# Hybrid attention layer: an early bias line, late weights a stage ahead, 128-row key blocks in B, A's mask on VectorE, one weight ring

## What is computed

```python
h  = rmsnorm(x, norm_g)                       # (1024 + 64) x 2048
qa, ka, va, qi, wi, ki, za, qb, kb, vb, zb, ga, gb = split(h @ w_in)
# A: 8 heads of 128, 2 kv heads. An indexer (16 heads of 64) scores every admissible key;
#    each query attends to its top 256 (prompt) of the keys; the sample also reads 2048 cached keys
score = sum_h relu(qi . ki) * wi ;  idx = top_k(score, n_sel)
oa = softmax(qa . ka[idx] * D_A**-0.5 + bias[t5_bucket(s - t)]) @ va[idx]
# B: 16 heads of 64, window of 128 keys back from the 64-frame chunk's start, plus the own chunk,
#    with a learned sink per head in the softmax, and the same T5 bias
ob = swa(qb, kb, vb, sinks, bias)
m  = sigmoid(ga) * ((oa * silu(za)) @ w_br_a) + sigmoid(gb) * ((ob * silu(zb)) @ w_br_b)
y  = rmsnorm(x + m @ w_out, final_g)
```

## Time and profile before

| | us |
|---|---|
| median of 3 runs (lowest, highest) | 3295.89 (3295.25, 3297.86) |
| the profiled execution | 3299.35 |
| its span | 3297.6 |
| PE busy | 3118.6 (95%), 17861 matmuls |
| DVE, ACT, POOL busy | 1321.4 (40%), 923.3 (28%), 1032.3 (31%) |
| mean granted clock of TensorE | 0.976 of full |

### The profile page before, as it was taken

One profiled execution on the slowest core, in us unless ns is written; L12 is line 12 of the kernel. 1 busy time (PEld: TensorE's weight loads), 2 busy tenths in 40 slices (PEclk: granted clock), 3 DMA queues, 4 the chain that ended last, 5 costly groups with the idle time before them and its releaser, 6 DMA issues. The chain is left out here.

```text
span 3297.6 us, 48426 instructions
## 1 busy us (share of the span) xinstructions
PE 3118.6 (95%) x17861; PEld 2950.5 (89%) x17861; DVE 1321.4 (40%) x2491; ACT 923.3 (28%) x1902; POOL 1032.3 (31%) x773
## 2 busy tenths in 40 slices
PE   6999999999999999889999799987998999899997
PEld 6999999999999989889999788876778999878776
DVE  6001563755567549900000256444873211120512
ACT  5111122121323131111111355444653111031423
POOL 1222211212222322222222366435762222143453
PEclk8999999999999999999999899997999999999998
DMA  4222222223232322153222553346545333263443
GB/s 159 66 79 77 73 65 73 71 68 84 71 100 74 98 73 80 54 141 99 80 80 82 147 152 101 93 106 153 118 97 178 104 125 105 79 224 98 150 160 105
DMA packets 432085, 341.57 MB, mean 104 GB/s; under 512 B 37244, under 2 KB 391644, under 8 KB 428428
## 3 DMA queue, kind: packets, MB, share of 16 engines
q1 hardware_dynamic: 398992, 275.97, 30.4%
q10 hardware_dynamic: 32956, 63.77, 6.0%
HBM read 264.25 MB, written 75.48 MB: 103 GB/s over the span
## 5 line engine op out<-in xcount | busy, mean ns | idle before, releaser
L466 POOL TENSOR_TENSOR w_in_tile_lo<-w_in_tile_raw,w_in_tile_hi 128x512 fp32r<-128x512 f32 x316 | 411.0, 1302 | 1391.4 <-ACT w_in_tile_hi L486 1391.4
L594 PE MATMUL banks<-h_early_hi,w_in_tile_hi 128*128 128x384 f32 x2496 | 639.4, 337 | 3.8 <-POOL w_in_tile_lo L466 3.8
L594 PE MATMUL banks<-h_early_hi,w_in_tile_lo 128*128 128x384 f32 x2496 | 636.5, 336 | 0.0
L594 PE MATMUL banks<-h_early_lo,w_in_tile_hi 128*128 128x384 f32 x2496 | 635.9, 336 | 0.0
L486 ACT CAST w_in_tile_hi<-w_in_tile_raw 128x512 fp32r<-128x512 f32 x316 | 196.3, 621 | 1254.1 <-PE banks L594 1128.5
L594 PEld LDWEIGHTS banks<-h_early_hi,w_in_tile_hi 128*128 128x128 f32 x2496 | 434.5, 188 | 13.0 <-issue 5.1
L594 PEld LDWEIGHTS banks<-h_early_hi,w_in_tile_lo 128*128 128x128 f32 x2496 | 434.8, 188 | 0.0
L594 PEld LDWEIGHTS banks<-h_early_lo,w_in_tile_hi 128*128 128x128 f32 x2496 | 434.4, 188 | 0.0
L761 DVE MAX8 top<-score 128x8 f32<-128x384 f32 (+6 forms) x224 | 247.2, 1103 | 33.0 <-DVE score L764 1.1
L764 DVE MATCH_REPLACE8 score<-top,score 128x384 f32<-128x384 f32 (+6 forms) x224 | 243.0, 1085 | 0.0
L2327 POOL TENSOR_TENSOR w_out_tile_lo<-w_out_tile_raw,w_out_tile_hi 128x512 fp32r<-128x512 f32 x128 | 173.7, 1360 | 215.4 <-ACT w_out_tile_hi L2337 215.4
(11 more groups left out here) (255 smaller groups left out, 5047.5 us busy)
## 6 DMA issues: line engine op xcount, KB each, us to landing
w_in_tile_raw<-in_w_in SPq DMA_DIRECT2D x440, 256.0 KB, 2.9
w_out_tile_raw<-in_w_out SPq DMA_DIRECT2D x128, 256.0 KB, 3.1
product<-spill ACTq DMA_DIRECT2D x46, 544.0 KB, 3.4
u_b<-product SPq DMA_DIRECT2D x32, 544.0 KB, 6.1
product<-spill ACTq DMA_DIRECT2D x32, 384.0 KB, 2.5
merged<-u_b ACTq DMA_DIRECT2D x16, 544.0 KB, 7.5
x_rows<-in_x_prompt SPq DMA_DIRECT2D x8, 1024.0 KB, 5.2
b_q_raw<-product SPq DMA_DIRECT2D x32, 256.0 KB, 4.8
```

The costliest lines, as they stand in the source:

```text
L466: pool.tensor_tensor(s.w_lo[:, q, :, :], s.w_raw[:, q, :, :], s.w_hi[:, q, :, :].bitcast(F32), ALU.subtract).then_inc(lo_made, 1)
L594: last = pe.matmul(ps[0:m, 3 * slot + c, 0:w], w_[:, q, kq, 0:m], tokens, start=(k == 0 and w_ is s.w_hi and h_ is s.h_hi), stop=(k == KT ...
```

## The change

1. The event `"bias line"` stands after the first tile of `QA`, with its two table DMAs issued at `"prompt keys"`. From the rows of A's heads their farthest value is subtracted (softmax doesn't change by a constant per row), so far keys need no bias: the far loads (L1011, L1356) go. The line is stored at once, on ACT's queue. What stood with it (the sample's mask, cache copies, the load of the sample's keys and values) is the new event `"load the sample"`, one tile later than `"bias line"` was.
2. The first two late tiles of each attention stage are loaded in the stage before (the second's DMAs at its end, `load_rest`), and the splits of the second wait for no load. The splits keep their points.
3. B's second key block has 128 rows: `prob` is padded with zero columns from 192 to 256 and the missing rows of `v_raw` with zeros; `values_lo` and the cast become one operation each.
4. The identity matmuls with A's mask go. Far pieces add the bf16 mask on DVE in place of the scalar; for near pieces POOL adds mask and bias beforehand, into a ring of 4 (`mask_near`, 64 operations in the prompt), or once in place (sample, at point 2). `load_mask` waits for `max_made` in place of `logits_done`.
5. All weight tiles use one set of buffers (`w_tile`). `attend_b` loads and splits merge's first branch tile after its last gate store, and `merge` loads and splits output's first four w_out tiles and loads its first two rows of m (`m_raw` becomes shared).
6. The fp32r and bf16 copies of the identity are not made.

```diff
     plan = [(QI, 2, "copy", None), "natural", (QI + 2 * P, 6, "copy", None), "prompt keys",
-            (QA, 2, "copy", None), (QA + 2 * P, 1, "copy", 2), (QA + 3 * P, 3, "copy", None),
+            (QA, 1, "copy", None), "bias line", (QA + P, 1, "copy", None), (QA + 2 * P, 1, "copy", 2), (QA + 3 * P, 3, "copy", None),
...
-            (GA + 20 * P, 2, "early", NB), (QB + 9 * P, 1, "copy", None), (GA + 22 * P, 8, "early", None),
-            "bias line", (GA + 30 * P, 2, "early", None),
+            (GA + 20 * P, 2, "early", NB), (QB + 9 * P, 1, "copy", None), (GA + 22 * P, 9, "early", None),
+            "load the sample", (GA + 31 * P, 1, "early", None),
...
                 elif what == "prompt keys":
+                    sp.dma_start(table, rel_bias).then_inc(consts_in, 16)
+                    sp.dma_start(hot, one_hot).then_inc(consts_in, 16)
...
-                elif what == "bias line":
+                elif what == "load the sample":
                     store_mask(NB)
-                    sp.dma_start(table, rel_bias).then_inc(consts_in, 16)
-                    sp.dma_start(hot, one_hot).then_inc(consts_in, 16)
...
-            load_tile(n_tiles, 0, 0, late_tile)
+            for k in range(2):
+                load_tile(n_tiles + k, 0, 0, late_tiles[k])
+            for q in range(QUARTERS):
+                sp.wait_ge(w_in_q[q], 16 * (n_tiles + 1))
...
+                    act.wait_ge(line_out, 3)
+                    act.dma_start(s.lines[:], line.unsqueeze(1).to_broadcast([H_A + H_B, P, RELS])).then_inc(line_stored, 16)
+                elif what == "load the sample":
...
+                    dve.memset(farthest, 0.0).then_inc(line_out, 1)
+                    dve.wait_ge(line_out, 1)
                     dve.wait_ge(line_done, 1)
-                    dve.tensor_copy(line, ps[0:H_A + H_B, 7, 0:RELS]).then_inc(line_out, 1)
-                    dve.wait_ge(line_out, 1)
+                    dve.tensor_copy(farthest[0:H_A, :], ps[0:H_A, 7, 0:1]).then_inc(line_out, 1)
+                    dve.wait_ge(line_out, 2)
+                    dve.tensor_scalar(line, ps[0:H_A + H_B, 7, 0:RELS], farthest, None, ALU.subtract).then_inc(line_out, 1)
...
+    def quarters(self, p, ahead, ready, end):
+
+        return range(*(max(ready, min(end, self.steps_before[x] // 4 + ahead)) if x >= 0 else ready for x in (p - 1, p)))
+
+    def load_quarter(self, sp, n):
+        t, q = divmod(n, QUARTERS)
+        sp.wait_ge(self.w_lo_made, n - 7)
+        src = self.w_in[0, q * KQ * P:(q + 1) * KQ * P, self.columns[t]:self.columns[t] + P]
+        sp.dma_start(self.s.w_raw[:, q, :, :], src.rearrange("(k p) c -> p k c", p=P)).then_inc(self.w_loaded[q], 16)
...
+        for n in self.quarters(p, 7, 2 * QUARTERS, QUARTERS * len(self.columns)):
+            self.load_quarter(sp, n)
+
+    def load_rest(self, sp):
+        end = QUARTERS * len(self.columns)
+        for n in range(min(end, self.steps_before[-1] // 4 + 7), end):
+            self.load_quarter(sp, n)
+        for q in range(QUARTERS):
+            sp.wait_ge(self.w_loaded[q], 16 * (len(self.columns) - 2))
...
+        for n in self.quarters(p, 4, QUARTERS, self.split):
             t, q = divmod(n, QUARTERS)
             act.wait_ge(self.w_used, n - 3)
-            act.wait_ge(self.w_loaded[q], 16 * t)
+            if t > 1:
+                act.wait_ge(self.w_loaded[q], 16 * (t - 1))
...
-                sp.wait_ge(logits_done, first_chunk[first_of(b - 1)])
+                sp.wait_ge(max_made, first_of(b - 1))
...
+            def mask_near(n):
+                b, u = units[n]
+                wide = min(NEAR, width[b])
+                if n == 0:
+                    pool.wait_ge(masks_set, 2)
+                if n in (0, PER):
+                    pool.wait_ge(table_in[n // PER], 16)
+                if u == 0 and b >= 2:
+                    pool.wait_ge(mask_in[b % 2], 16 * (b // 2))
+                if n >= RING:
+                    pool.wait_ge(max_made, n - RING + 1)
+                pool.tensor_tensor(near_masked[:, n % RING, 0:wide], near[:, u, NEAR - wide:NEAR], mask[:, b % 2, width[b] - wide:width[b]],
+                                   ALU.add).then_inc(near_made, 1)
...
+                mask_near(p)
+            mask_near(START)
             for n in range(len(units)):
                 if n == 0:
                     scale(0)
                 if n in values_at:
                     values_lo(values_at.index(n))
                 scale(n + 1)
+                if n + RING < len(units):
+                    mask_near(n + RING)
...
-                            t0 = NEAR - width[units[n][0]] + at
-                            last = dve.tensor_tensor_reduce(out=out, in0=acc, in1=near[:, u, t0:t0 + wide], scale=1.0, scalar=TAKEN,
-                                                            op0=ALU.add, op1=ALU.max, accum_out=top)
...
+                            t0 = min(NEAR, width[b]) - width[b] + at
+                            added = near_masked[:, n % RING, t0:t0 + wide]
                         else:
-                            last = dve.tensor_scalar(out, acc, far[:, u:u + 1], None, ALU.add, ALU.max, accum_out=top)
+                            added = mask[:, b % 2, at:at + wide]
+                        last = dve.tensor_tensor_reduce(out=out, in0=acc, in1=added, scale=1.0, scalar=TAKEN, op0=ALU.add,
+                                                        op1=ALU.max, accum_out=top)
...
-                    pe.matmul(acc, s.ident_b[:, :], mask[:, b % 2, c0:c0 + w], start=True, stop=False)
                     for q_, k_ in ((q_hi, k_hi), (q_hi, k_lo), (q_lo, k_hi)):
-                        last = pe.matmul(acc, q_[:, b % 2, u * P:(u + 1) * P], k_[:, kv, c0:c0 + w], start=False,
-                                         stop=q_ is q_lo)
+                        last = pe.matmul(acc, q_[:, b % 2, u * P:(u + 1) * P], k_[:, kv, c0:c0 + w],
+                                         start=q_ is q_hi and k_ is k_hi, stop=q_ is q_lo)
...
+                if p == 2:
+                    pool.wait_ge(table_in, 32)
+                    pool.wait_ge(mask_in, 32)
+                    pool.tensor_tensor(near[:, :, :], near[:, :, :],
+                                       mask[:, KEYS_S - NEAR_W:KEYS_S].unsqueeze(1).to_broadcast([P, UNITS, NEAR_W]),
+                                       ALU.add).then_inc(near_made, 1)
...
-            return W_S, [(CACHED, P, 0), (OWN, CHUNK, P)]
+            return W_S, [(CACHED, P, 0), (OWN, P, P)]
         if b == 0:
             return (half + 1) * CHUNK, [(0, (half + 1) * CHUNK, 0)]
-        return W_S, [(half * ODD + b - 1, P, 0), (half * ODD + b, CHUNK, P)]
+        return W_S, [(half * ODD + b - 1, P, 0), (half * ODD + b, P, P)]
...
-        prob = sb("prob", [P, RING, PAIRS, W_S])
+        prob = sb("prob", [P, RING, PAIRS, NEAR])
...
+            gates.load_rest(sp)
+            for q in range(QUARTERS):
+                sp.wait_ge(gates.w_lo_made, QUARTERS * (len(columns) - 1) - 3 + q)
+                load_branch_quarter(sp, s, w_br_a, w_br_b, slice(0, P), q, br_in[q])
...
+            pool.memset(prob[:, :, :, W_S:NEAR], 0.0).then_inc(padded, 1)
+            pool.wait_ge(padded, 1)
+            pool.memset(v_raw[CHUNK:P, OWN - 1:OWN + 1, :], 0.0).then_inc(padded, 1)
+            pool.wait_ge(padded, 2)
...
+            for q in range(QUARTERS):
+                pool.wait_ge(br_hi_made, q + 1)
+                pool.tensor_tensor(s.w_lo[:, q, :, :], s.w_raw[:, q, :, :], s.w_hi[:, q, :, :].bitcast(F32),
+                                   ALU.subtract).then_inc(br_lo_made, 1)
+            pool.wait_ge(br_lo_made, QUARTERS)
...
+            for q in range(QUARTERS):
+                act.wait_ge(gates.w_used, QUARTERS * (len(columns) - 1) + q + 1)
+                act.wait_ge(br_in[q], 16 * (KV_B if q < 2 else 1))
+                act.copy(s.w_hi[:, q, :, :], s.w_raw[:, q, :, :]).then_inc(br_hi_made, 1)
             gates.finish(act)
...
+            for k in range(2):
+                sp.wait_ge(m_stored[k], 16)
+                sp.dma_start(s.m_raw[:, k, :], s.mT[k * P:(k + 1) * P, 0:FIRST_TOKENS]).then_inc(next_in, 16)
+            for k in range(4):
+                sp.wait_ge(lo_made, TILES * 4 + (k - 3))
+                sp.dma_start(s.w_raw[:, k, :, :].rearrange("p a c -> p (a c)"), w_out[0, k * P:(k + 1) * P, 0:512]).then_inc(
+                    w_out_in[k], 16)
+            sp.wait_ge(next_in, 32)
...
+            pool.sem_inc(lo_made, QUARTERS)
+            split_lo(1)
+            with pool.Fori(1, TILES // 2) as i:
                 for j in range(2):
                     split_lo(i * 2 + j)
+            split_lo(TILES)
+            pool.wait_ge(lo_made, TILES * 4 + 4)
...
+                act.wait_ge(w_used, TILES * 4 + (k - 3))
+                act.wait_ge(w_out_in[k], 16)
+                act.copy(s.w_hi[:, k, :, :], s.w_raw[:, k, :, :]).then_inc(hi_made, 1)
...
+                if k < 4:
```

(32 more changed lines are left out.)

177 lines of the change are left out of this document (74 added, 103 removed).

## The result

The changed kernel takes 3266.56 us (median of 4 runs, 3264.57 to 3273.02) against 3296.36 before (4 runs, 3295.25 to 3297.86): ratio 0.9905, 95% interval 0.9894 to 0.9917, 29.8 us faster. I had forecast 3243, 53 faster, with a range up to 3264; the time lies above it. The profiled execution has a span of 3266.2.

What follows compares the result with a forecast made beforehand. TensorE, busy 95% of the span, was taken as the bound. Terms summed to −53.0 from the profiled 3299.35 us, giving 3246.35, or 3243 us by the median measure; range about ±12, down to 3227 and up to 3264.

Steps and rivals of the forecast that it cites:

- The line's store moved early: Project stage: storing the line's 4608 KB beside the weights of copy tiles costs +0.5 us (0 to +3) through contention.
- own sign of being wrong: Project stage: shrinking by less than 12 us would show the prediction wrong, with the moved line costing weights.
- the ring's four quarters, some 17 us: Project stage: products on weight quarters already loaded, some 17 us, were to cover the line's transfer.
- The hole at the bias line: Project, around 1410 us: TensorE's hole of 21.97 us shrinks to 4.6, waiting for weights; term −16.2 (−17.5 to −13).
- The prompt's attention: Whole stage −9.8 us: −5.5 at its start from weights loaded ahead, +0.7 at its end, −5 from the mask.
- The mask term: Prompt's attention: 16.1 us of mask products leave TensorE, most given back through POOL's additions; −5 (bounds −13 and +5).
- POOL pacing the stage: Rival, prompt's attention: POOL's additions set the pace, mask term +5 rather than −5; 3253 us (3248 to 3260), chance 0.16.
- The sample: Sample's attention: mask products and the wait for the mask's DMA leave TensorE; −6.5 us (−9 to −3).
- B and its start: B's start: preloading removes the 7.2 us wait for the fourth weight quarter, −7 (−9.5 to −2); B to merge −16.
- The 128 rows: B's second key block: products start 0.24 apart in place of 0.33 and 0.34; −6 us (−8.5 to 0).
- The barrier's delay at B's end: B to merge: POOL's four subtractions and the casts at B's end delay the barrier some 3.7 us; whole term −3.
- Merge to output: Output's start: the 13.4 us wait shrinks as weights and m are in place at the barrier; −5 us (−6 to −3).

## Why the prediction was right and where it failed

*The failed step: "The line's store moved early ... +0.5 (0 to +3)".* The prediction's own sign of being wrong came true: the project stage shrank by 2.6 us, where less than 12 was to mean that the moved line costs weights. It cost 15 to 19 us by the timed runs, 15.7 by the shift of the trace (the indexer's waits near 547 before stand at 562.7 after). I had costed the transfer against the ring of weights as it stands in undisturbed work, and VectorE's small operations at their durations. Neither costs by itself, as the two runs with one of them alone show. What I left out is the wait that the change adds on VectorE: behind it stood the cast of the first queries, behind that SyncE's second query load, and behind that four weight quarters, which used up the cover that I counted on just when the transfer began. The cover was "the ring's four quarters, some 17 us", and the quarters came 16.6 us late into it (296.9 instead of 280.3).

*The hole at the bias line* was right to 0.2 us: 4.4 left, at 1426.8 for the shift of 15.7 (4.6 forecast; 1390.71 + 16.7 is 1407.4 and not 1407.2, which makes 4.4), and 4.4 to 4.5 in the second profile and in the runs with the line elsewhere.

*The prompt's attention*: −5.9 in the first profile, −10.7 in the second, −10.2 and −10.3 with the line elsewhere, for −9.8. The mask term is right by the medians and 3 small by the stage. Its working is not: I had 16.1 gained (the products as listed sum to 16.3) and 11 given back by POOL's additions; these give back 3.6, and some 4 go into waits for VectorE, which I had at nothing. That the term came out near is in part luck. The likeliest rival, POOL pacing the stage (0.16), is out.

*The sample*: −7.7 to −7.9 in three profiles and −2.8 to −6.0 in the others (the run with one tile ahead apart), for −6.5. In the three, PE's longest wait for the maxima of a chunk (chunk_max_s) is 1.6 to 1.7 us, in all the others 4.0; what makes it one or the other was not tried.

*B and its start*: the holes in front shrank from 2.6 and 7.2 to 1.9 and 3.1, 4.8 for a forecast of 7. The 128 rows give 4 to 6 for 6, but not as I had it: PE's work shrinks by 7.8 and the wait for POOL's stacked queries grows by 3.9, a term that the sum lacks. B to its end plus merge give 15.3 and 15.1 in the two profiles of the changed kernel and 18.5 with the store late, for 21. The barrier's delay at B's end was forecast at 3.7; POOL ends 5.2 behind PE's last product, and PE's wait is 8.9 for 7.3. This stage is the second part of the miss: −9.6 and −9.1 for −16.

*Merge to output*: 13.4 to 8.8, 4.6 for 5.

With the loss at the line avoided, the sum is nearly met: 51 us (3296 × 0.0155) with the store moved late and 48 with the line computed early, for 53. So the one step is the miss by its size. But the terms meet their sum partly by luck: in the profile with the store late, B gave 8.1 for 16 and the sample 4.2 for 6.5, against 18.8 for 15.7 up to the prompt's attention and 10.4 for 5 in merge.

## What to carry to other kernels

When an event moves in a written order, list for every engine what now stands behind its wait, and follow it through the queues to the DMAs, before counting the cover that a large transfer needs: a delay and a burst that each cost nothing cost their meeting. A transfer that nobody needs soon goes where no loads are behind schedule; computing early and storing later are two decisions. And a named wait is not yet a gain: three orders, each aimed at one, gained nothing, and two of them only showed the wait that stood behind it. Work taken off PE is a gain only as far as the engines that feed it are ahead: of 7.8 us in B half was waited away, of 16 in the prompt half.

## What the runs showed of the hardware that I had not expected

A 256 KB weight quarter that lands about 3 us after its issue (2.9 median) was cast 18 us after it when issued 5 us into a transfer of 4608 KB, and the next ones came 4 us apart; the DMA engines were busy 0.81 to 0.86 at 193 to 211 GB/s in the windows shown. An addition of f32 and bf16 operands on GpSimd takes 679 ns for 128x256, no more than the 736 of the f32 form. Taking the maximum with a bf16 tensor added costs VectorE 501 ns on average over 64 operations, where the scalar form took 562. Changing from products of 128 rows to products of 64 cost 0.10 and 0.11 us on the next two starts; between two products of 64 rows the spacing was the 0.23 of 128 rows.
